# Compression with the blocks stationary in column halves, first scores moved ahead of it, and retention values made by token

## The reference, cut to what matters

```python
def compress_blocks(kv, pe, w1, w2):              # kv: S x 2 x 64
    blocks = kv[tok_idx] + pe[None, :, None, :]   # 31 blocks of 32 tokens
    flat = blocks.transpose(0, 2, 1, 3).reshape(n_cmp, G, CMP_LEN * dh)
    return jax.nn.gelu(flat @ w1) @ w2            # 2048 -> 256 -> 64
...
g = jax.nn.sigmoid(gi.astype(jnp.float32))
o = g[..., 0:1] * o_c + g[..., 1:2] * o_s + g[..., 2:3] * o_w
```

## Time and profile before

| | us |
|---|---|
| median of 3 runs (2006.74 to 2007.55) | 2007.41 |
| profiled execution, its own time | 2005.59 |
| its span, first to last instruction | 2003.4 |
| PE busy in the span | 1958.6 |
| DVE, ACT, POOL busy | 1128.3, 850.7, 81.8 |
| mean granted TensorE clock | 0.995 |

### The profile page before, as it was taken

How to read it: one execution, slowest core, us unless ns; L and a number is a source line. 1 busy time by engine, 2 the same in 40 slices (tenths; PEclk the granted TensorE clock), 3 DMA queues, 4 the chain that set the end, 5 groups by cost and what they waited for, 6 DMA issues and landing times.

```text
span 2003.4 us, 25728 instructions
## 1 busy us (share of the span) xinstructions
PE 1958.6 (98%) x10336; PEld 1591.7 (79%) x10336; DVE 1128.3 (56%) x1853; ACT 850.7 (42%) x1486; POOL 81.8 (4%) x99
## 2 busy tenths in 40 slices
PE   8999999999999999999999999999999999999997
PEld 6767777788888888888877777888898788888886
DVE  5567765644455444422637888885655465444323
ACT  4155532533444222222427777784435453222221
POOL 0000000000010000000200000011100020000000
PEclk9999999999999999999999999999999999999998
DMA  7111111223323222232221111113233222222231
GB/s 282 54 33 53 54 63 53 85 89 105 98 67 106 95 95 95 89 95 91 86 84 64 64 64 54 53 43 105 74 117 115 85 74 95 95 95 92 87 97 61
DMA packets 49430, 170.53 MB, mean 85 GB/s; under 512 B 5520, under 2 KB 8080, under 8 KB 48928
## 3 DMA queue, kind: packets, MB, share of 16 engines
q1 hardware_dynamic: 48816, 166.73, 25.5%
q0 software_dynamic: 496, 2.16, 0.3%
HBM read 166.77 MB, written 2.10 MB: 84 GB/s over the span
## 4 chain that ended last, share of the span: by engine, by line
PE 91%; DVE 5%; ACT 2%; issue 1%; DMA 0%; SPq 0%; DVEq 0%
PE acc L1802 58%; PE bank L1802 18%; PE bank L1891 2%; PE bank L2103 1%; PE acc L2303 1%; PE bank L1964 1%; PE bank L2138 1%; PE bank L2039 1%; DVE bank L1158 1%; PE bank L1937 1%; DVE w_lo L1078 1%; PE bank L2290 1%; PE bank L2324 1%; DVE residual L1164 1%; PE bank L1824 1%
## 5 line engine op out<-in xcount | busy, mean ns | idle before, releaser
L1078 DVE TENSOR_TENSOR w_lo<-w_raw,w_hi 128x1024 fp32r<-128x1024 f32 (+2 forms) x306 | 365.9, 1198 | 305.1 <-ACT w_hi L578 304.7
L1802 PE MATMUL acc<-act_hi,w_hi 128*128 128x512 f32 (+1 forms) x1160 | 457.9, 395 | 17.4 <-DVE w_lo L1078 9.6
L1802 PE MATMUL acc<-act_lo,w_hi 128*128 128x512 f32 (+1 forms) x1160 | 444.8, 383 | 0.0
L1802 PE MATMUL acc<-act_hi,w_lo 128*128 128x512 f32 (+1 forms) x1160 | 444.8, 383 | 0.0
L578 ACT ACTIVATE w_hi<-w_raw 128x1024 fp32r<-128x1024 f32 (+2 forms) x306 | 314.4, 1029 | 211.4 <-PE acc L1802 180.9
L1802 PEld LDWEIGHTS acc<-act_hi,w_hi 128*128 128x128 f32 x1160 | 218.5, 188 | 72.2 <-issue 17.4
L1802 PEld LDWEIGHTS acc<-act_hi,w_lo 128*128 128x128 f32 x1160 | 218.5, 188 | 46.9
L1802 PEld LDWEIGHTS acc<-act_lo,w_hi 128*128 128x128 f32 x1160 | 218.8, 189 | 45.4 <-issue 2.2
L1802 PE MATMUL bank<-act_hi,w_hi 128*128 128x512 f32 (+1 forms) x520 | 192.7, 370 | 1.2 <-DVE w_lo L1078 1.2
L1802 PE MATMUL bank<-act_lo,w_hi 128*128 128x512 f32 (+1 forms) x520 | 191.0, 367 | 0.0
L1802 PE MATMUL bank<-act_hi,w_lo 128*128 128x512 f32 (+1 forms) x520 | 190.9, 367 | 0.0
(11 more groups left out here) (452 smaller groups left out, 3012.3 us busy)
## 6 DMA issues: line engine op xcount, KB each, us to landing
w_raw<-w_all SPq DMA_DIRECT2D x282, 512.0 KB, 3.3
w_raw<-w_all SPq DMA_DIRECT2D x16, 384.0 KB, 3.1
residual<-xT SPq DMA_DIRECT2D x8, 256.0 KB, 7.7
cmp_w_k<-w1k SPq DMA_DIRECT2D x1, 2048.0 KB, 8.0
cmp_w_v<-w1v SPq DMA_DIRECT2D x1, 2048.0 KB, 12.2
w_raw<-w_all SPq DMA_DIRECT2D x8, 256.0 KB, 2.6
out_t<-residual SPq DMA_DIRECT2D x16, 128.0 KB, 1.7
ret_decay<-decay POOLq DMA_DIRECT2D x4, 256.0 KB, 3.2
```

Source lines behind the costliest of these rows:

```text
L1078: TT(WL[:, c % RAW_RING, 0:nb * P], WR[:, c % RAW_RING, 0:nb * P], WH[:, c % HI_RING, 0:nb * P].bitcast(F32), ALU.subtract).then_inc(s_lo, 1)
L1802: ins = MM(bank[:, cols], w[:, at, k * P:(k + 1) * P], x, start=first and r == 0 and k == 0, stop=last and r == 2 and k == nb - 1)
```

## The change

- **Compression.** `BLK` has 64 columns (62 blocks and two of zeros) and is the stationary side; the 256 weight columns move. Keys go to partitions 0 to 63 of a bank, values to 64 to 127, in turn. The hidden layer comes out block by feature and is evicted as one gelu, turned by PE in two pieces and copied by ACT (`HID`, `HT`) ahead of the second layer.
- **The value blocks** `BLK["v"]` are written by GpSimd, one instruction after the other.
- **Order.** The first selected and window scores go ahead of the compression, with their maxima and exps. The gate rows are cut in pieces of 6, 1 and 1 steps around it. The value turns go behind it, with ACT instead of DVE as copier, and one step of `ret_in` is made ahead of the first turn.
- **Gates.** ACT makes exp(-x), DVE adds one, and the sums are multiplied by it before the reciprocal.
- **Maxima.** In each block the compressed maximum comes after the window ones, waiting for them.
- **Retention values** are made token by feature: `HH`, `HL` pieces of 128 tokens stationary, two slots' weights (256 columns) moving, as 16 steps of three. ACT evicts 128x256 pieces twice, first scaled by -1/256 with a sum (the mean), then with that mean as bias. `RV`'s turns and `centre_values` are gone. The two slots are free together. `ret_in_split` says which slot is split at which block.
- **Retention's first head** has half of its first `z_ret` tile between scores and value products.

```diff
@@ gpsimd
+            for t in ("k", "v"):
+                nc.gpsimd.memset(BLK[t][:, :, 2 * N_CMP:64], 0.0).then_inc(sem("cmp_blocks_v"), 1)
+            pool.wait_ge(s_in, 48)
+            wait_apart(pool, s_acc, TILE0["nsa_plain"] + 1, sem("pool_seen"))
+            pool.wait_ge(sem("cmp_blocks_v"), 2)
+            for n, ins in enumerate(compression_blocks(nc.gpsimd.tensor_tensor, "v", VN[:, 0, :])):
+                ins.then_inc(sem("cmp_blocks_v"), 1)
+                pool.wait_ge(sem("cmp_blocks_v"), 3 + n)
@@ scalar
+        def ret_in_split(u):
+            return None if u == SC - 1 else SLOT0["ret_in"] + u + (AHEAD if u < SC else AHEAD - 1)
...
+            def compress():
+                act.wait_ge(sem("cmp_hidden"), 1)
+                A(HID[:], PS[4][:, 0:CMP_HIDDEN], ACT.Gelu_apprx_tanh).then_inc(sem("cmp_gelu"), 1)
+                act.wait_ge(sem("cmp_hidden"), 2)
+                A(HT[:], PS[4][:, CMP_HIDDEN:2 * CMP_HIDDEN].rearrange("p (j c) -> p j c", j=2), ACT.Copy).then_inc(
+                    sem("cmp_gelu"), 1)
+                act.wait_ge(sem("gate_sum"), 1)
+                A(GT[:], GT[:], ACT.Exp, scale=-1.0).then_inc(sem("gate_exp"), 1)
...
-                dst = EV[:, s, :] if s < 2 else RV[:, p * 2 + s - 2, :]
-                A(dst, ACC[(TILE0["ret_in"] + s) % 2][:], ACT.Copy).then_inc(s_acc, 1)
+                for n, dst, made in parts:
+                    ins = A(dst, made, ACT.Copy, scale=-1.0 / RET_DV, accum_out=RVM[:, n:n + 1])
+                ins.then_inc(sem("ret_v_means"), 1)
+                act.wait_ge(sem("ret_v_means"), p * 2 + s - 1)
+                for n, dst, made in parts:
+                    ins = A(dst, made, ACT.Identity, bias=RVM[:, n:n + 1])
+                ins.then_inc(s_acc, 1)
@@ vector
+            def cmp_max():
+                chain.link(V.reduce_max(MX[:, 0:2], PS[4][:, 0:64].rearrange("p (h c) -> p h c", h=2)[:, :, 0:N_CMP], AX))
+                TS(NM[:, 0:2], MX[:, 0:2], -NSA_SCALE, None, ALU.mult).then_inc(sem("nsa_win_max"), 1)
...
-                    chain.link(V.reciprocal(SR[:], SU[:]))
-                    chain.link(TT(SW[:].rearrange("q (b h) -> q b h", h=2), SR[:].rearrange("q (b h) -> q b h", h=2), gates,
+                    chain.link(TT(SR[:].rearrange("q (b h) -> q b h", h=2), SU[:].rearrange("q (b h) -> q b h", h=2), gates,
                                   ALU.mult))
+                    chain.link(V.reciprocal(SW[:], SR[:]))
...
-            split_lo(SLOT0["ret_in"] + NSA_PAIRS * SC - 1 + AHEAD)
+            split_lo(ret_in_split(NSA_PAIRS * SC - 1))
+            split_lo(SLOT0["z_ret"] + AHEAD - 1)
@@ tensor
+            def ret_values(p, part, steps):
+                c, tile = SLOT0["ret_in"] + 4 * p + 2, TILE0["ret_in"] + 4 * p + 2 + part
+                if steps[0] == 0:
+                    pe.wait_ge(s_lo, c + 2)
+                    pe.wait_ge(s_acc, tile - 1)
+                for j, k in (divmod(step, DK) for step in steps):
+                    out = acc_bank("ret_in", 4 * p + 2 + part)[:, j * RET_DV:(j + 1) * RET_DV]
+                    at = slice((2 * part + j) * P, (2 * part + j + 1) * P)
+                    for r, (w, ring, a) in enumerate(((WH, c % HI_RING, HH), (WL, c % RAW_RING, HH), (WH, c % HI_RING, HL))):
+                        ins = MM(out.rearrange("p (e f) -> p e f", e=2), a[:, k, at], w[:, ring:ring + 2, k * P:(k + 1) * P],
+                                 start=r == 0 and k == 0, stop=r == 2 and k == DK - 1)
...
+            def compressed():
+                for b in range(16):
+                    for n, t in enumerate(("k", "v")):
+                        ins = MM(PS[4][64 * n:64 * n + 64, 0:CMP_HIDDEN], BLK[t][:, b, :], W1[t][:, b, :], start=b == 0,
+                                 stop=b == 15)
+                return ins
+
+            def first_scores():
+                pe.wait_ge(sem("nsa_roped"), 6)
+                wide_scores(0, 0, 0).then_inc(sem("nsa_sel_scored"), 1)
+                pe.wait_ge(sem("gate_w_lo"), 1)
+                narrow_rows(5, WGH, WGL, 24, range(0, 6))
+                pe.wait_ge(sem("nsa_roped"), COUNT["nsa_rope"])
+                wide_scores(0, 0, 1).then_inc(sem("nsa_first_win_scored"), 1)
+                pe.wait_ge(s_late["cmp_w"], 64)
+                pe.wait_ge(sem("cmp_blocks_k"), 1)
+                pe.wait_ge(sem("cmp_blocks_v"), 10)
+                compressed().then_inc(sem("cmp_hidden"), 1)
+                narrow_rows(5, WGH, WGL, 24, range(6, 7))
+                pe.wait_ge(sem("cmp_gelu"), 1)
+                for j in range(2):
+                    ins = TR(PS[4][:, CMP_HIDDEN + j * P:CMP_HIDDEN + (j + 1) * P], HID[:, j * P:(j + 1) * P], ident)
+                ins.then_inc(sem("cmp_hidden"), 1)
+                narrow_rows(5, WGH, WGL, 24, range(7, DK)).then_inc(sem("gate_rows"), 1)
+                pe.wait_ge(sem("cmp_gelu"), 2)
...
+                ins.then_inc(sem("cmp_done"), 1)
+                pe.wait_ge(sem("gate_rows_copied"), 1)
+                token_major(5, 24).then_inc(sem("gate_psum"), 1)
+                pe.wait_ge(s_acc, TILE0["nsa_plain"] + 3)
+                turn(None, VN[:, 2, :], SC).then_inc(sem("nsa_v_turned"), 1)
+                pe.wait_ge(sem("nsa_masks"), 1)
+                pe.wait_ge(sem("cmp_kv"), 1)
+                cmp_scores(0, 0).then_inc(sem("nsa_win_scored"), 1)
+                pe.wait_ge(sem("gate_sum"), 1)
+                turn(5, VN[:, 1, :], SC).then_inc(sem("nsa_v_turned"), 1)
+                ret_in(0, 0, range(0, 1))
...
-            pe.wait_ge(s_acc, TILE0["z_ret"])
-            def ret_turn_values(h):
-                for e in range(2):
-                    turn(ret_v_bank(e), RV[:, h * 2 + e, :], SC).then_inc(sem("ret_v_turned"), 1)
-
-            ret_turn_values(0)
+            pe.wait_ge(sem("nsa_out"), NSA_PAIRS)
             pe.wait_ge(sem("ret_roped"), 2 + 8)
...
+                else:
+                    gemm("z_ret", 0, HH, HL, half=0)
+                    pe.wait_ge(s_acc, TILE0["z_ret"])
...
-                if h + 1 < RET_HEADS:
-                    ret_turn_values(h + 1)
-                gemm("z_ret", 2 * h, HH, HL)
+                gemm("z_ret", 2 * h, HH, HL, half=None if h else 1)
```

More of the change, by code:

```diff
@@ L446, in ssd_x, with compression_blocks @@
             return XT[:, n - 4, :] if n >= 4 else XB[:, n + 4, :]
+        def compression_blocks(add, t, src):
+            for g in range(2):
+                kv = src[64 * g:64 * g + 64, :].rearrange("p (m b r) -> p m b r", b=8, r=2)
+                for r in range(2):
+                    for a in range(2):
+                        pe_at = PCOL["pe_" + t][0] + r * 16 + a * 8
+                        yield add(BLK[t][64 * r:64 * r + 64, 8 * a:8 * a + 8, g * N_CMP:(g + 1) * N_CMP],
+                                  kv[:, a:a + N_CMP, :, r].rearrange("p m b -> p b m"),
+                                  PA[64 * g:64 * g + 64, pe_at:pe_at + 8].unsqueeze(2).broadcast_to([64, 8, N_CMP]),
+                                  ALU.add)
         @block.sync
@@ L760, in _ @@
                     act.wait_ge(sem("nsa_sel_max"), u + 1)
-                    for hh in range(2):
-                        A(PB[:, hh, 0:kw], PS[hh][:, 0:kw], ACT.Exp, bias=NM[:, 2 + hh:3 + hh], scale=NSA_SCALE,
-                          accum_out=SU[:, 2 + hh:3 + hh])
+                    far_exps(0, kw)
+                    if u == 0:
+                        act.wait_ge(sem("nsa_first_win_max"), 1)
+                        far_exps(1, kw)
+                        compress()
                     act.wait_ge(sem("nsa_win_max"), u + 1)
-                    for hh in range(2):
-                        A(PB[:, 2 + hh, 0:kw], PS[2 + hh][:, 0:kw], ACT.Exp, bias=NM[:, 4 + hh:5 + hh], scale=NSA_SCALE,
-                          accum_out=SU[:, 4 + hh:5 + hh])
+                    if u:
+                        far_exps(1, kw)
                     for hh in range(2):
@@ L1348, in hide_later, with far_max @@
                 return TT(block, block, const("causal"), ALU.add)
+            def far_max(branch, i):
+                hide_later(2 * branch, i)
+                chain.link(hide_later(2 * branch + 1, i))
+                for hh in range(2):
+                    at = 2 * branch + hh
+                    ins = V.reduce_max(MX[:, 2 + at:3 + at], PS[at][:, 0:(i + 1) * P], AX)
+                chain.link(ins)
+                return TS(NM[:, 2 + 2 * branch:4 + 2 * branch], MX[:, 2 + 2 * branch:4 + 2 * branch], -NSA_SCALE, None,
+                          ALU.mult)
@@ L1350, in _, with maxima @@
+            def maxima(u, i):
+                dve.wait_ge(sem("nsa_sel_scored"), u + 1)
+                far_max(0, i).then_inc(sem("nsa_sel_max"), 1)
+                dve.wait_ge(sem("nsa_win_scored"), u + 1)
+                far_max(1, i)
+                cmp_max()
+            first_maxima()
             for p in range(NSA_PAIRS):
@@ L1871, in done, with narrow_rows @@
```

(15 more changed lines are left out.)

210 lines of the change are left out of this document (85 added, 125 removed).

## The result

The changed kernel takes 1991.99 us (median of 4 runs, 1991.31 to 1992.22), the one before 2007.08 us beside it (4 runs, 2006.24 to 2007.55): a ratio of 0.9925, 95% interval 0.9913 to 0.9937, 15.1 us less. The forecast was 1990.9, range 1987.5 to 1997.5. The profiled execution has a span of 1990.0 us (2003.4 before) and an own time of 1991.78 (2005.59 before). The sum was made against these two, so it is read first: it said -16.5, the spans differ by -13.4 and the own times by -13.8.

The account below looks back on a forecast made before the run. TensorE was taken to bound the kernel, waiting mainly at the first block's attention and the retention's start. -13.3 (first block) + 1.0 (clock) + 1.0 (middle) - 5.2 (retention) = -16.5, from 2007.41 to 1990.9 us, range 1987.5 to 1997.5.

Parts of the forecast that it names:

- The compression: First block: key and value column halves work at once, 7.3 us instead of 14.6, so 7.3 gained; ends 6.9 and 13.8.
- Rival (a): Compression: the halves take turns or their weight loads stand between, +6.5 us, so 1997.4; chance 0.07.
- The chain behind it: First block, after compression: 5.05 us to the mask of compressed probabilities, then 1.68 to the first turn at 94.05.
- the one on the block copies: Before compression: value blocks move to GpSimd, hidden, done by 76.7; DVE gets 4.3 us back and first scores do not wait.
- Rival (b): Block copies: GpSimd is late, contending with DVE; at 2.8 us each compression starts 7 us later, 1998; chance 0.06.
- From the first turn to the second: First block: 8.5 us instead of 8.93, recovering the block's slack; second turn at 102.6 instead of 115.90.
- The clock: Around the first turn: a possible fall to half rate after PE's idle time, taken as 1.0 us cost, 0 to 2.5.
- The middle: Middle blocks: compressed maximum waits 0.12 us in eight blocks, ACT's evictions 0 to 0.3 in three places; cost 1.0, 0 to 2.5.
- Rival (c): Middle blocks: ACT's evictions and the later maximum cost 0.6 us in each of 15 blocks, +8, 1999; chance 0.05.
- The retention: Retention's start: half a gate tile fills the wait, 2.8 us; no turns for three next heads, 2.4; gain 5.2, 3.5 to 5.5.
- Rival (d): Retention values: 256-column matmuls do not cover their 188 ns weight load, +27 us, so 2018, slower; chance 0.02.
- Rival (e): First block's wait moves elsewhere and the retention's DVE order eats that gain: near 2004 us; chance 0.03.

Follow-up runs that it names:

- experiment 3: The changed kernel with all sixteen key products of the compression first, then all sixteen value products, instead of alternating: 1996.43 us, 0.9948 of the kernel before.
- Experiments 1: The changed kernel without GpSimd's eight value block additions, the value side of the compression working on zeros: 1989.51 us, 0.9914 of the kernel before.
- experiment 2: The changed kernel with GpSimd starting the value blocks only when DVE's key blocks are done: 1989.12 us, 0.9916 of the kernel before.
- experiment 10: The changed kernel with 18 gate products ahead of the selected scores and the compressed maximum back ahead of the window ones: 1990.74 us, 0.9921 of the kernel before.
- Experiment 6: The changed kernel with three steps of the retention's input ahead of the first turn instead of one: 1990.76 us, 0.9918 of the kernel before.
- experiment 4: The changed kernel with the compressed maximum of blocks 1 to 15 back ahead of the window maxima: 1989.36 us, 0.9913 of the kernel before.
- experiment 7: The changed kernel with ACT evicting each retention value tile in one copy, without centring: 1990.97 us, 0.9918 of the kernel before.

## Why the prediction was right

By its own terms, against the profiled executions:

| term | forecast | measured |
|---|---|---|
| first block to the second turn, clock included (-13.3 + 1.0) | -12.3 | -10.2 |
| middle blocks | +1.0 | +1.6 |
| retention, first head -2.8, turns of three heads -2.4 | -5.2 | -5.4 |
| start of the whole trace (+0.7), and the rest (-0.1) | 0 | +0.6 |
| span | -16.5 | -13.4 |

The first line is the 9.53 and the 0.68 by which this execution ran late at 75 us already; the last but one is those 0.68 less a rest of 0.1 that belongs to no part of the change. The span came 3.1 us short of the forecast. Medians, 15.1 and 16.6 us below the kernel before, lie nearer to it, since the profiled execution of before was 1.5 us below its median (2007.08) and that of after only 0.2. That the median hit within 1.1 us is in part luck: it comes from the draw of the profiled executions, while the first line of the table missed by 2.1.

**The compression** is as the prediction read it: 7.05 us against 7.3, and the records of a half start 0.215 us apart, so a pair costs 0.43 to 0.44 and the loss of 0.04 seen in the earlier trace rows is hardly there with 256 columns. Rival (a) is out: experiment 3 shows what the halves cost one after the other, 13.15 us, where the prediction had 13.8. The Trainium skill (TensorEngine Tiling (Array Packing), Restrictions under Tile-to-Partition Mapping) has it that column tiling turns the fast weight load off; the trace shows no cost of it, since the loads (0.13 to 0.14 us each) lie beside the products: 0.215 us from record to record is all there is.

**The chain behind it** was forecast at 6.75 us from the last compression product to the first turn, and took 6.87. The selected and window scores and the 18 gate products took 0.35 more than the 4.75 they were given. The first turn came at 96.16, where 94 was forecast.

**The step that failed** is the one on the block copies: "DVE gets 4.3 us back", and the first scores without a wait. The prediction asked only whether GpSimd would be late. It was not: eight additions at 0.94 us, less than the 1.47 taken. But the two engines hold each other up, and DVE got back 4.31 less 2.35 (key blocks) less 0.52 (rotation), 1.4 us. PE waits 1.11 us for the sixth rotated tile. Experiments 1 and 2 show cause and price, 1.15 us; experiment 10 that the price is PE's wait. Rival (b) named the contention, but on the wrong side of it. It also took all of DVE's additions from 63 to 79 us to have two SBUF inputs; `nsa_v` (from `acc`) and `tmp_a` (from `bank`) have one in PSUM. The Trainium skill (SBUF — State Buffer, Who interferes with whom) states it: a DVE instruction with two SBUF inputs contends with a GpSimd instruction that reads SBUF. The trace agrees, 0.69 to 1.21 us with two SBUF inputs and 0.69 unchanged with one; but it also has two SBUF inputs at an unchanged 0.68 where DVE's instruction had started first, and then GpSimd's grew (experiment 2).

**From the first turn to the second** 8.5 us was forecast at full clock. It is 9.02: the scaling's slack of 0.45 was not there to recover, since both the start and the end of that stretch hang on DVE (PE waits 0.26 to 0.29 ahead of the second turn as it is). Experiment 6 shows the same from the other side.

**The clock**: 1.0 was taken, with 0 and 2.5 as bounds. It cost 1.2 us in the profiled execution, nothing in six others, and 2.7 in the worst, a little over the bound. The prediction had named a clock under 1.00 after 97 us as a sign of being wrong, and the profiled execution shows it, 97.1 to 100.6. The term covers it, so it is the sign that was badly chosen. That the forecast of 1.0 lies near the 1.2 of this one execution is luck, since the same kernel shows both 0 and 1.2; that was not foreseen.

**The middle** was the right mechanism, mis-sized: the compressed maximum behind the others costs 1.4 us (experiment 4), not 8 x 0.12 = 1.0. In a pair, the distance from second to third turn grew from 10.23 to 10.45 and from third to fourth from 11.77 to 11.93, four times 0.38. ACT's evictions cost nothing (experiment 7). Rival (c) had both at 0.6 us in each of 15 blocks, and is out.

**The retention** is right in each part: the first value product stands 4.95 us behind the end of the input products (271.64 less 266.69), where the forecast had 5.0, and PE has no pause before it. Rival (d), uncovered weight loads, is out by the spacing of 0.117 us. Rival (e), waits that only move, held in small: PE's 1.11 us at the first scores, and the wait that experiment 6 moved.

## What to carry to other kernels

When work is handed to another engine, cost it twice: what the receiver needs, and what it does to every instruction that runs beside it, then see whether someone waits behind those. Before a wait is filled, look for what sets the next one; a chain that depends on its own last result (scores, maxima, exps, scaling) gives nothing back to a filler ahead of it. And take a kernel's profile twice before a difference of a microsecond is read as an effect of the edit.

## What the runs showed of the hardware

- DVE and GpSimd additions side by side: DVE's eight of 64x248 take 6.66 us instead of 4.31, of which the six beside GpSimd start 0.93 us apart and the two after it 0.5; its 128x512 sum of two SBUF tiles goes from 0.69 to 1.21. GpSimd's eight take 7.55 us beside the key blocks and 9.73 beside other DVE work, with single ones from 0.73 to 1.70. In the rows looked at singly, the one that starts second is held up by the other, whichever engine it is (experiment 2). The move still saves DVE time: 7.2 us of block additions and slower rotation instead of 8.6.
- Two column halves of the array at work at once lose almost nothing with 256 f32 columns moving: 0.44 us for a pair (7.05 over 16), 0.43 for one alone. For that they have to alternate in the program: with all keys ahead of all values, the same 32 products took 13.15 us, and the halves ran together only for the 0.6 us where one group meets the other.
- The granted clock behind a pause of 1.6 us differs between executions of the same kernel with the same work before it: it stayed at full in one profile, and was low for 3.4 us in another; in a kernel with the gate rows first it was low for 6.8. With a pause of only 0.24 us at the first turn it stayed in both profiles taken; two are too few for a rule.
